# Compressed-branch scores of an attention layer: block keys made the stationary operand, in column groups, and turned back to token rows

## What is computed

```
kc = _compress(k_c, w_ck)                                  # [B, 8, G, D]
vc = _compress(v_c, w_cv)
s = jnp.einsum('btgrd,bngd->bgrtn', qg, kc) * SCALE
mask = ((blk + 1) * CMP_BLOCK - 1)[None, :] <= q_pos[:, None]
p = _masked_probs(s, mask)
o = jnp.einsum('bgrtn,bngd->btgrd', p, vc)                 # later times the gate g[..., 0, :]
```

## Time and profile before

| | |
|---|---|
| median of three runs | 1247.75 us (1247.19 to 1249.63) |
| profiled execution | 1249.45 us; span of its trace 1247.7 us; the other 1.7 us lie around it |
| busy share of the span | PE 95%, PEld 86%, DVE 40%, POOL 37%, ACT 30% |
| mean granted TensorE clock | 0.978 |

### The profile page before, as it was taken

How to read it: one execution, slowest core, us unless ns; L and a number is a source line. 1 busy time by engine, 2 the same in 40 slices (tenths; PEclk the granted TensorE clock), 3 DMA queues, 4 the chain that set the end, 5 groups by cost and what they waited for, 6 DMA issues and landing times.

```text
span 1247.7 us, 20962 instructions
## 1 busy us (share of the span) xinstructions
PE 1179.6 (95%) x8618; PEld 1078.1 (86%) x8618; DVE 504.4 (40%) x643; ACT 371.4 (30%) x497; POOL 465.4 (37%) x257
## 2 busy tenths in 40 slices
PE   6899998999999999898999889999999999999996
PEld 5899998999999998565564449999999999999995
DVE  5585672044312121767974343444323232300115
ACT  5113433223211113444433322334322222222211
POOL 5232554466333411116511023344344434434440
PEclk9899999999999989998999999999999999999997
DMA  5532126333523210750015272332332232222201
GB/s 179 153 95 69 51 84 203 102 101 107 181 68 101 80 28 1 274 159 18 18 35 171 77 272 68 102 102 68 101 101 70 98 101 85 83 94 94 92 25 69
DMA packets 108785, 124.10 MB, mean 99 GB/s; under 512 B 10478, under 2 KB 102662, under 8 KB 107455
## 3 DMA queue, kind: packets, MB, share of 16 engines
q1 hardware_dynamic: 105544, 118.61, 30.4%
q10 hardware_dynamic: 3191, 4.80, 1.2%
HBM read 111.38 MB, written 16.17 MB: 102 GB/s over the span
## 4 chain that ended last, share of the span: by engine, by line
PE 75%; issue 13%; POOL 5%; DVE 5%; DMA 2%; ACT 1%; POOLq 0%; DVEq 0%; SPq 0%; ACTq 0%
PE D L1667 53%; PE E L1667 6%; PE D L1913 5%; POOL w_lo L692 4%; PE D L1899 1%; PE D L1901 1%; PE D L1900 1%; PE E L1986 1%; DMA w_raw<-in_w_in 1%; DVE nmax L1394 1%; PE E L1824 1%; PE E L1884 1%; DVE obuf L1422 1%; PE E L1927 1%; PE D L1861 1%
## 5 line engine op out<-in xcount | busy, mean ns | idle before, releaser
L692 POOL TENSOR_TENSOR w_lo<-w_raw,w_hi 128x1024 fp32r<-128x1024 f32 x164 | 402.2, 2474 | 577.6 <-ACT w_hi L770 535.2
L770 ACT ACTIVATE w_hi<-w_raw 128x1024 fp32r<-128x1024 f32 x164 | 164.1, 1049 | 288.4 <-PE D L1667 244.0
L1667 PE MATMUL D<-hH,w_hi 128*128 128x260 f32 x1152 | 237.0, 288 | 7.7 <-POOL w_lo L692 5.5
L1667 PE MATMUL D<-hH,w_lo 128*128 128x260 f32 x1152 | 235.1, 286 | 0.0
L1667 PE MATMUL D<-hL,w_hi 128*128 128x260 f32 x1152 | 234.9, 286 | 0.0
L1667 PEld LDWEIGHTS D<-hH,w_hi 128*128 128x128 f32 x1152 | 181.4, 193 | 8.9 <-POOL w_lo L692 5.7
L1667 PEld LDWEIGHTS D<-hL,w_hi 128*128 128x128 f32 x1152 | 180.9, 192 | 0.0
L1667 PEld LDWEIGHTS D<-hH,w_lo 128*128 128x128 f32 x1152 | 180.9, 192 | 0.0
L1667 PE MATMUL D<-onH,w_hi 128*128 128x260 f32 x832 | 168.5, 284 | 1.1 <-DVE onL L1574 1.1
L1667 PE MATMUL D<-onH,w_lo 128*128 128x260 f32 x832 | 168.4, 284 | 0.0
L1667 PE MATMUL D<-onL,w_hi 128*128 128x260 f32 x832 | 168.3, 284 | 0.0
(11 more groups left out here) (344 smaller groups left out, 1578.7 us busy)
## 6 DMA issues: line engine op xcount, KB each, us to landing
w_raw<-in_w_in SPq DMA_DIRECT2D x64, 512.0 KB, 5.0
w_raw<-in_w_ffn_in SPq DMA_DIRECT2D x44, 512.0 KB, 4.4
slot<-in_cache_kv SPq DMA_DIRECT2D x64, 128.0 KB, 2.9
w_raw<-in_w_ffn_out SPq DMA_DIRECT2D x16, 512.0 KB, 4.4
rows_b<-rnorm_d SPq DMA_DIRECT2D x8, 512.0 KB, 4.7
w_raw<-in_w_nsa_out SPq DMA_DIRECT2D x8, 512.0 KB, 7.0
slot<-in_cache_win SPq DMA_DIRECT2D x16, 256.0 KB, 4.7
w_raw<-in_w_o SPq DMA_DIRECT2D x8, 512.0 KB, 3.9
```

What stands on the lines that cost most here:

```text
L692: nc.gpsimd.tensor_tensor(wl[b][:, x], raw[b][:, x], wh[b][:, x].bitcast(F32), ALU.subtract)\
L770: nc.scalar.activation(wh[b][:, x], raw[b][:, x], ACT.Copy).then_inc(hi_done, 1)
L1667: ins = mm(out2[:, a, 0:HALF], lhsT, rhs[:, a * HALF:(a + 1) * HALF], start=first, stop=last)
```

## The change

- The block keys lie in `kc_pad`, 48 columns per half `f`: 16 of zeros, 8 + 8 of keys, 16 of zeros. They are the stationary operand now, 32 columns at a time, and the queries of all 512 tokens move: 8 matmuls, one for each feature tile `t`. Matmul `t` writes 32 partitions of `E[:, 0]`, group `t // 2`; even `t` takes (keys, zeros) and odd `t` (zeros, keys), so two matmuls that accumulate fill a group. Groups are visited as 0, 1, 2, 3, 0, 1, 2, 3.
- The scores now stand in rows of (head, block). DVE copies them to `th[:, 1]`, and four transposes on PE bring them back to token rows in `E[:, 1]`, from which the softmax goes on.
- DVE's copy of the block values stands behind that new copy.
- Heads now come in the order of the tiles (`f, r, j`), so the gate product and `vbig` are two instructions each.

```diff
+        kc_pad = smalls[:, :, :].rearrange("p a c -> p (a c)")[:, 256:352].rearrange("p (f c) -> p f c", f=2)
...
-                nc.vector.tensor_copy(kc_blk[rows, :, j * NBLK:(j + 1) * NBLK], kc_sum[rows, 0:2, :])\
-                    .then_inc(cmp_sums, 1)
+                c = 2 * NBLK + j * NBLK
+                nc.vector.tensor_copy(kc_pad[rows, :, c:c + NBLK], kc_sum[rows, 0:2, :]).then_inc(cmp_sums, 1)
+            dve.wait_ge(cmp_scores, 1)
+            nc.vector.tensor_copy(th[:, 1, 0:SEQ], E[:, 0, :]).then_inc(cmp_sums, 1)
             dve.wait_ge(vc_turned, 1)
             vc_tok = tmp[0:NBLK, 1, 0:KVC]
             nc.vector.tensor_copy(vc_tok, E[0:NBLK, 2, 0:KVC]).then_inc(vc_evac, 1)
-            dve.wait_ge(cmp_scores, 1)
+            dve.wait_ge(cmp_scores, 2)
...
-            nc.vector.tensor_tensor(cs, E[:, 0, :].rearrange("p (q h k) -> p q h k", q=QT, k=NBLK),
+            nc.vector.tensor_tensor(cs, E[:, 1, :].rearrange("p (q h k) -> p q h k", q=QT, k=NBLK),
...
+            for f in range(2):
+                step(nc.vector.tensor_tensor(ct[:, f, :, :, :], ct[:, f, :, :, :], gt[:, f, :, :, :, 0], ALU.mult))
...
+            for f in range(2):
+                nc.vector.tensor_tensor(vbig_g[:, f, :, :, :], vc_g[:, f, :, :].unsqueeze(2).to_broadcast(full),
+                                        own[:, f, :, :].unsqueeze(3).to_broadcast(full), ALU.mult).then_inc(vbig_ready, 1)
...
-            for q in range(QT):
-                for t in range(KT):
-                    ins = mm(csv[:, q, t // R, t % R, :, :], qT[:, t, q * P:(q + 1) * P],
-                             kc_blk[:, t // R, :].rearrange("p (j k) -> p j k", j=2), start=True, stop=True)
+            for t in (0, 2, 4, 6, 1, 3, 5, 7):
+                rows, o = slice(t // 2 * 32, t // 2 * 32 + 32), 2 * NBLK * (1 - t % 2)
+                ins = mm(E[rows, 0, :], kc_pad[:, t // R, o:o + 32], qT[:, t, 0:SEQ], start=(t % 2 == 0), stop=(t % 2 == 1))
             ins.then_inc(cmp_scores, 1)
             pe.wait_ge(vc_evac, 1)
             mm(E[:, 3, 0:KVC], rep[:, :, :].rearrange("p h k -> p (h k)"), tmp[0:NBLK, 1, 0:KVC],
                start=True, stop=True).then_inc(vc_rep, 1)
+            pe.wait_ge(cmp_sums, 3)
+            for q in range(QT):
+                ins = turn(E[:, 1, q * P:(q + 1) * P], th[:, 1, q * P:(q + 1) * P], ident[:, :])
+            ins.then_inc(cmp_scores, 1)
...
-                    pe.wait_ge(vbig_ready, 1)
+                    pe.wait_ge(vbig_ready, 2)
```

More of the change, by code:

```diff
@@ L279, in build @@
         E = ctx.enter_context(nc.psum_tensor("E", [P, 4, 512], F32))
-        kc_sum = smalls[:, 5, 0:32].rearrange("p (n k) -> p n k", n=4)
+        kc_sum = smalls[:, 5, 32:64].rearrange("p (n k) -> p n k", n=4)
+        kc_pad = smalls[:, :, :].rearrange("p a c -> p (a c)")[:, 256:352].rearrange("p (f c) -> p f c", f=2)
         kcs = smalls[:, 3, 0:2 * NS * NBLK_S]
@@ L287, in build @@
         o_own = tmp[:, 1, 0:2 * DH]
-        kc_blk = smalls[:, 4, 0:32].rearrange("p (f c) -> p f c", f=2)
         x_landed = [sem(f"x_landed{q}") for q in range(QT)]
@@ L1349, in _ @@
             settle()
-            gt = gates_tok[:, :, :].rearrange("p q (h c) -> p q h c", c=3)
-            step(nc.vector.tensor_tensor(crc.rearrange("p (q h) -> p q h", q=QT),
-                                         crc.rearrange("p (q h) -> p q h", q=QT), gt[:, :, :, 0], ALU.mult))
+            gt = gates_tok[:, :, :].rearrange("p q (f j r c) -> p f q r j c", f=2, j=2, c=3)
+            ct = crc.rearrange("p (q f r j) -> p f q r j", q=QT, f=2, j=2)
+            for f in range(2):
+                step(nc.vector.tensor_tensor(ct[:, f, :, :, :], ct[:, f, :, :, :], gt[:, f, :, :, :, 0], ALU.mult))
             settle()
@@ L1357, in _ @@
             dve.wait_ge(pe_done, 2 * C_NSA)
[L1358 to L1362, removed]
+            full = [P, 2, R, DH]
+            own = headmask[:, :].rearrange("p (f r j) -> p f j r", f=2, j=2)
+            vbig_g = vbig[:, :].rearrange("p (f j r d) -> p f j r d", f=2, j=2, r=R)
+            vc_g = E[:, 3, 0:KVC].rearrange("p (f j d) -> p f j d", f=2, j=2)
+            for f in range(2):
+                nc.vector.tensor_tensor(vbig_g[:, f, :, :, :], vc_g[:, f, :, :].unsqueeze(2).to_broadcast(full),
+                                        own[:, f, :, :].unsqueeze(3).to_broadcast(full), ALU.mult).then_inc(vbig_ready, 1)
             dve.wait_ge(pc_turned, 1)
@@ L1820, in _ @@
             pe.wait_ge(gates_ready, 2)
-            csv = E[:, 0, :].rearrange("p (q f j r k) -> p q f r j k", q=QT, f=2, j=2, r=R)
-            for q in range(QT):
-                for t in range(KT):
-                    ins = mm(csv[:, q, t // R, t % R, :, :], qT[:, t, q * P:(q + 1) * P],
-                             kc_blk[:, t // R, :].rearrange("p (j k) -> p j k", j=2), start=True, stop=True)
+            for t in (0, 2, 4, 6, 1, 3, 5, 7):
+                rows, o = slice(t // 2 * 32, t // 2 * 32 + 32), 2 * NBLK * (1 - t % 2)
+                ins = mm(E[rows, 0, :], kc_pad[:, t // R, o:o + 32], qT[:, t, 0:SEQ], start=(t % 2 == 0), stop=(t % 2 == 1))
             ins.then_inc(cmp_scores, 1)
```

## The result

The changed kernel takes 1241.22 us in the median of 18 runs (1237.43 to 1246.90), the kernel before 1249.53 in 18 runs beside them (1244.03 to 1254.81): a ratio of 0.9932, with a 95% interval of 0.9919 to 0.9946, so some 8.3 us faster. 1236.2 was forecast, with a range up to 1241.0: the sign is right, the gain 3.2 us too large, the time just outside. The profiled execution is 1240.48, its span 1238.8.

The account below looks back on a forecast made before the run. PE, busy 95% of the span, was taken as the bound, with the scores wholly on its path. 8.82 (earlier chunk 36) + 2.88 (dense work) - 0.15 (`vbig`) = 11.55 us gave 1236.2, range 1233.5 to 1241.0.

Parts of the forecast that it names:

- the base: Median of the kernel before, 1247.75 us, from which the forecast time was taken; the profiled execution was 1249.45.
- the stretch: PE's first gate transpose behind chunk 35 to its first probabilities transpose: chunk 36 starts 8.82 us earlier, dense work saves 2.88.
- 16 passes: Scores, eight matmuls of 512 columns: four groups overlap fully, 1.72 us plus a tail of 0.16.
- From the last score to the spreading matmul: PE waits for DVE's two copies before L1828: 0.04 + 0.68 + 0.41 + 0.06 us.
- the spreading matmul and the transposes: L1828 and four new transposes ahead of chunk 36, at full clock: 0.57 + 0.44 us.
- `vbig` lost: Product on the chain, split into two halves: 1.38 us instead of 1.24, 0.15 lost; at worst 0.5.
- the rival of a falling clock: Scores to dense work: clock falls all the same, gain 7.7 us, time 1240.1; chance 0.15.
- the dense work's 2.88 us as a constant: Four chunks behind the scores, 384 rows: 46.12 us instead of 49.00 if the clock holds.
- Further on the whole program moves forward as it is.: Work after the changed place keeps its length; one low-clock stretch more or less makes 1.6 us either way.
- Less overlap: Scores: groups overlap only in pairs, time 1239.6 by gain 9.83 against 1249.45, stated as 1237.9; none, 1241.4; chance 0.15.
- the slower one: Scores: groups do not overlap and the clock falls, 13.74 us for 16 passes, time 1252.1; chance 0.03.
- no gain: Time saved is waited away before chunk 38 or in the attention behind, about 1247; chance 0.03.

Follow-up runs that it names:

- `b_filler`: Kernel before with two matmuls that nothing reads behind each of the 32 score matmuls, 64 in all: 1260.64 us.
- `b_filled_wait`: Kernel before with 64 unread matmuls among the scores and 14 more ahead of PE's wait for the block keys: 1252.38 us, 1.0017 of before.
- `b_again`: Kernel before, nothing edited, run again for a second profile; 62.1 us from the gate transpose behind chunk 35 to the probabilities' first transpose, no own median given.
- `a_unrolled`: Changed kernel with chunks 36 and 37 written out instead of in PE's loop, nothing else: 1237.87 us, ratio 0.9911 against the kernel before.

## Why the prediction was wrong, step by step

The time came out 5.0 us above the forecast. Of that, 1.8 is the base, 0.8 the stretch, which was dearer in the profile of before than in the mean of four (the dense work by 0.6, the scores by 0.2), and 2.4 is gain in the stretch that did not arrive at the end.

**Right: the stretch.** Worked on the profile of before, chunk 36 was to move from 14.7 to 5.9 us behind chunk 35 and did (14.73 and 5.91, a gain of 8.82 as summed; the terms below miss by 0.02, 0.11 and 0.03, so the exact agreement is luck); the dense work was to take 46.12 and took 46.14. Within it: 16 passes (MATMUL rows) in 1.90 with their tail, forecast 1.88, so four groups run side by side without loss. The estimate from the Trainium skill's figure of 2.38 times for three column tiles ("TensorE: Matmul & The Clock Gate", section "Measured speedup vs the span model") was 2.17 without the tail; the trace, with 1.74 without it, does not agree. From the last score to the spreading matmul PE waited 1.08 instead of 1.19, as DVE's second copy starts under the first's end; the spreading matmul and the transposes 1.04 until chunk 36 (432.93 to 433.97) instead of 1.01. `vbig` lost 0.06 instead of 0.15 (1.30 against 1.24).

**Right: the clock** stayed at 1.00 over the transposes and the wait for DVE; the rival of a falling clock did not happen in any of the profiles with the change. The Trainium skill, in the section "PE-mode transpose" of "TensorE: Matmul & The Clock Gate", says that transposes don't count as busy for the clock, which spoke for that rival. The trace is against it: 1.00 over the four transposes (428.25 to 434.00) and over the mostly transposed work of the earlier trace rows.

**In part: why the clock fell before.** The prediction put it down to passes of few columns ("a listed-busy PE that streams little does not keep its clock"). But in the profile of `b_filler` the clock fell with longer matmuls among them, and in `b_filled_wait` it held once the wait ahead was filled too, so the wait has a part that the prediction did not give it.

**Wrong in size: the dense work's 2.88 us as a constant.** "384 would take 46.12 instead of 49.00" is true of one execution. The chains of four profiles of before have 49.00, 47.89, 48.25 and 48.65, so the term is 1.8 to 2.9. The scores before vary too (10.9 to 12.1), and the whole stretch gives 9.9 to 11.5, 10.7 in the mean. The sum took one draw of a cost that varies with the clock, near its dear end.

**Wrong: "Further on the whole program moves forward as it is."** Of the 10.7 us, 7.6 to 8.4 arrive in the medians of four comparisons (7.9 to 9.5 in the means), so some 1 to 3 us are given back. They are not in the stretch. The eight profiles put the program behind chunk 39 at 758.2 us before and 760.5 after in the mean, which fits the amount, but each set scatters by 4 to 7 us, and over all twenty profiles, edited kernels included, it is 759.0 and 759.7. What is shown is the scatter: in the eight profiles the way from the end of chunk 39 to the sample stage takes 204.1 to 209.4 us and the sample stage 47.4 to 52.4, where the transfer and the clock both have a part. Nor does a low-clock stretch cost "about half its length" wherever it falls: the first profile of before has one of 3.5 us in its sample stage (mean clock 0.96) and takes 47.8 us, `b_again` has none (1.00) and takes 47.5. Why the later stages cost one kernel more than the other is **open**: it is not the distance moved alone (unrolling moved nothing, and the time fell by 1 to 3 us), not PE's loop alone (before gained nothing), not that transfer (6.1 us in the mean of nine profiles of before and its edits, 6.1 in eleven of the changed kernel and its edits), and not how much low clock there is in all: the five runs of `a_unrolled` have a mean clock of 0.980 to 0.981, the changed kernel's 18 a median of 0.981. The prediction allowed 1.6 us either way for this.

**The base.** The prediction subtracted from 1247.75, the median of three runs; eighteen have 1249.53. The measured gain, 8.3 us, lies inside the gains that the range stood for (6.75 to 14.25 us); it is this 1.8 us that put the time above 1241.0.

**Rivals.** Less overlap did not happen: 1.90 us, not 3.6 or 7. Nor did the slower one, with a lone group at half clock. Of "no gain", time that is waited away further on, only the 1 to 3 us above may be a small part, and no run shows a wait that holds them.

## What to carry to other kernels

Here a PE that was listed busy with 64 passes of 16 columns, behind a short wait, ran most of them at half clock, and the dense work behind paid as well. Swapping the operands, so that the long side moves, and putting results of 32 rows into different column groups, where they ran side by side, took away both costs. When the price of a stretch depends on the clock, read it from several profiles, since one gives one draw, and take the base from more than three runs when the kernel's own executions spread over 10 us. And once PE waits for a copy by DVE, put other PE work into that wait: moving four transposes behind the next chunk took DVE out of that stretch of the chain.

## What the runs showed of the hardware that was not expected

- Sixteen fp32 passes of 512 columns in four column groups take 1.90 us, 16 with a full stationary operand 6.87; the order of the passes changes nothing (1.95 against 1.92).
- Adding 78 matmuls (9.3 us of work) to a stretch of 62.8 us made it 1.4 us longer, because the clock stayed at 1.00 instead of 0.50; 64 of them without the 14 in the wait ahead left the clock at 0.50 for 23.75 us and more in the profile taken.
- The same sample stage, with the same busy time on DVE, ACT and POOL, takes 47.4 or 52.4 us from one execution to the next, with mean clocks of 0.96 and 0.87, and 50.5 at 0.97 where a transfer on the chain took 6.95 us instead of 5.27.
- Writing two chunks out instead of looping made the changed kernel 1 to 3 us faster and the kernel before not at all; no run here explains it.
